# Output projection, norms and gate/up projection in one block, in token halves

## The reference

```python
hp = hp + rms_norm(mp, nw[1])
hs = hs + rms_norm(ms, nw[1])
hp = hp + rms_norm(swiglu(rms_norm(hp, nw[2]), ffn_w_gu[layer], ffn_w_down[layer]), nw[3])
hs = hs + rms_norm(swiglu(rms_norm(hs, nw[2]), ffn_w_gu[layer], ffn_w_down[layer]), nw[3])
```

## Time and profile before

| | us |
|---|---|
| median of 3 runs (1813.19 to 1816.3) | 1814.0 |
| the profiled execution | 1809.09 |
| its span, first to last instruction | 1807.4 |
| TensorE's matmuls busy in it | 1622.2 |

### The profile page before, as it was taken

One profiled execution on the slowest core, in us unless ns is written; L12 is line 12 of the kernel. 1 busy time (PEld: TensorE's weight loads), 2 busy tenths in 40 slices (PEclk: granted clock), 3 DMA queues, 4 the chain that ended last, 5 costly groups with the idle time before them and its releaser, 6 DMA issues. The chain is left out here.

```text
span 1807.4 us, 40950 instructions
## 1 busy us (share of the span) xinstructions
PE 1622.2 (90%) x16700; PEld 1511.5 (84%) x16700; DVE 811.6 (45%) x1344; ACT 498.0 (28%) x901; POOL 479.3 (27%) x406
## 2 busy tenths in 40 slices
PE   6998986999984999998997799999896999998994
PEld 5997974565584999998997799999695999998994
DVE  3332205565655444433233777675456344442334
ACT  3110004455532222221121433323233222221220
POOL 0001114576601344443000234342001444442001
PEclk9999798999996999998999899999798999999997
DMA  9655678687540222222221134343120222222211
GB/s 279 196 172 201 237 271 336 218 252 223 156 154 24 76 89 92 93 93 93 95 85 56 59 107 119 106 130 95 47 94 24 94 93 92 85 94 96 89 56 48
DMA packets 82982, 226.68 MB, mean 125 GB/s; under 512 B 17918, under 2 KB 18608, under 8 KB 81282
## 3 DMA queue, kind: packets, MB, share of 16 engines
q1 hardware_dynamic: 77522, 210.09, 35.4%
q0 software_dynamic: 3392, 11.02, 1.7%
q10 hardware_dynamic: 1936, 3.74, 0.6%
HBM read 206.28 MB, written 23.77 MB: 127 GB/s over the span
## 5 line engine op out<-in xcount | busy, mean ns | idle before, releaser
L370 PE MATMUL gu_ps<-gu_x_hi,gu_w_hi 128*128 128x260 f32 x1408 | 288.4, 286 | 38.3 <-DVE gu_x_lo L336 31.3
L370 PE MATMUL gu_ps<-gu_x_hi,gu_w_lo 128*128 128x260 f32 x1408 | 285.3, 284 | 0.0
L370 PE MATMUL gu_ps<-gu_x_lo,gu_w_hi 128*128 128x260 f32 x1408 | 284.8, 284 | 0.0
L370 PEld LDWEIGHTS gu_ps<-gu_x_hi,gu_w_hi 128*128 128x128 f32 x1408 | 219.7, 190 | 41.1 <-issue 40.0
L370 PEld LDWEIGHTS gu_ps<-gu_x_hi,gu_w_lo 128*128 128x128 f32 x1408 | 218.7, 190 | 0.0
L370 PEld LDWEIGHTS gu_ps<-gu_x_lo,gu_w_hi 128*128 128x128 f32 x1408 | 218.0, 189 | 0.0
L289 DVE TENSOR_TENSOR gu_w_lo<-ring,gu_w_hi 128x1024 fp32r<-128x1024 f32 x88 | 143.8, 1634 | 100.5 <-ACT gu_w_hi L262 100.5
L370 PE MATMUL down_ps<-ffn_h_hi,down_w_hi 128*128 128x260 f32 x704 | 143.7, 286 | 17.2 <-DVE down_w_lo L289 17.2
L1239 POOL TENSOR_SCALAR arena<-arena 128x128 f32<-128x128 f32 (+3 forms) x128 | 137.1, 1087 | 79.0 <-DVE arena L1370 78.9
L456 POOL TENSOR_TENSOR ffn_h_hi<-ffn_a,ffn_g 128x520 f32 (+1 forms) x44 | 59.4, 1349 | 319.7 <-DVE ffn_g L445 319.7
L370 PE MATMUL down_ps<-ffn_h_lo,down_w_hi 128*128 128x260 f32 x704 | 142.7, 284 | 0.0
(11 more groups left out here) (337 smaller groups left out, 2899.4 us busy)
## 6 DMA issues: line engine op xcount, KB each, us to landing
ring<-in_w_gu SPq DMA_DIRECT2D x88, 512.0 KB, 3.7
ring<-in_w_down SPq DMA_DIRECT2D x32, 704.0 KB, 4.0
arena<-in_cache_cmp SPq DMA_DIRECT2D x86, 256.0 KB, 5.0
ring<-in_hgrn_w_in SPq DMA_DIRECT2D x32, 512.0 KB, 3.9
X<-in_slc_kv SPq DMA_DIRECT2D x48, 256.0 KB, 3.4
ring<-in_nsa_w_in SPq DMA_DIRECT2D x21, 512.0 KB, 3.8
arena<-in_cache_cmp POOLq DMA_DIRECT2D x42, 256.0 KB, 5.6
ring<-in_slc_kv SPq DMA_DIRECT2D x40, 256.0 KB, 3.1
```

The source lines that it names most:

```text
L370: last = pe.matmul(ps[j][:, h, 0:TH], wt[:, s % 2, a], xt[:, x, h * TH:(h + 1) * TH], start=(sub == 0 and k == 0 and part == 0), stop=(sub ...
```

## The change

The output projection, the norm after the mixer, the norm before the feed-forward part and gate/up become one block per layer, `mix_ffn`. Output tiles 0 to 3 are computed as before. Tiles 4 to 7 are computed for the first 260 tokens, and then all four for the second 260, from four slots of split weights; two of these lie in memory of the hidden units that are written last. While TensorE is at the second halves, the first half of the tokens goes through the norm. Gate/up tiles 0 to 2 follow in the same way, first for half 0, then for half 1; tile 3 is the first for all tokens, and from tile 4 on the loop is as before. Every operation of both norms is on 260 columns, except the mean and root of the second norm. The squares of the output are made by ScalarE from PSUM and added by GpSimd, and GpSimd makes all additions to `X`. In layer 0 the queries lie in `XW`, and the attention's output is written over them; the input projection is written out without a loop for this. The clearing of semaphores after the mixer now comes ahead of the output projection.

```diff
+def repeat(eng, first, last, unrolled):
+
+    if unrolled:
+        yield from range(first, last)
+    else:
+        with eng.Fori(first, last) as i:
+            yield i
...
-                with eng.Fori(1, loops) as i:
+                for i in repeat(eng, 1, loops, unrolled):
...
+        eng.tensor_tensor(pairs((c.XW[:, n, :] if n < KC else HT[:, n - KC, :])), ps[j][:, :, 0:TH], pairs(c.rstd[:, :]),
+                          ALU.mult).then_inc(c.psum_free[j], 1)
...
+def mix_ffn(c, name, w_mix, w_gu, nxt, Y, post_w, scale, hidden, ffn, ssq, x_ready=None):
...
+    PRE, ROUNDS = 3, 2 * FF // RING
...
+        late = FF * T - 4 * KC * P
+        more_h, more_l = [carve(flat_h, late + x * 2 * KC * P, 2, KC * P) for x in range(2)]
+        sh, sl = [carve(flat_l, x * KC * T, KC, T) for x in range(2)]
...
+        mq = [c.ring[:, 2 * x:2 * x + 2, KC * P:KC * P + TH] for x in range(2)]
+        w_hi, w_lo = [[x[:, 0, :], x[:, 1, :], m[:, 0, :], m[:, 1, :]] for x, m in ((wh, more_h), (wl, more_l))]
...
+            for tile in range(8):
+                s = tile % RING
+                sp.wait_ge(c.lo_cut[s], done[s] + tile // RING + 1)
+                load_tile(sp, c, w_mix if tile < RING else w_gu, s, (tile + RING) % KC, KC)
...
+                    used(act, n)
+                    act.activation(mq[n % 2], ps[j][:, :, 0:TH], ACT.Square).then_inc(mixed_sq, 1)
+                    act.activation(pairs(Y[:, n, :]), ps[j][:, :, 0:TH], ACT.Copy).then_inc(c.psum_free[j], 1)
...
+            cut(-8, 0)
+            for k in range(KC):
+                act.activation(sh[:, k, :], Y[:, k, :], ACT.Copy).then_inc(s_hi, 1)
+            for n in range(1, RING):
+                cut(n - 8, n)
...
+            for n in range(RING):
+                if n == 0:
+                    act.wait_ge(s_lo, KC)
+                out(n)
+                cut(n - RING, n)
+            for n in range(RING, 8):
+                out(n, 0)
+            out(4, 1)
+            root(1, cols[0])
+            used(act, 4)
+            cut(0, 0)
+            for k in range(2):
+                x_cut(0, k)
+            out(5, 1)
+            used(act, 5)
+            cut(1, 1)
+            for k in range(2, 4):
+                x_cut(0, k)
+            out(6, 1)
+            used(act, 6)
+            cut(2, 2)
+            for k in range(4, 6):
+                x_cut(0, k)
+            out(7, 1)
+            used(act, 7)
+            cut(3, 3)
+            for k in range(6, KC):
+                x_cut(0, k)
+            for k in range(4):
+                square(0, k)
+            root(2, cols[1])
+            for k in range(4, KC):
+                square(0, k)
+            for k in range(KC):
+                x_cut(1, k)
+                square(1, k)
+            root(3, slice(0, T))
+            later(act, cut)
...
+            def mean(h):
+
+                dve.wait_ge(summed, h + 1)
+                own.link(dve.tensor_scalar(c.rstd[:, cols[h]], ps[3][:, h, 0:TH], 1.0 / D_MODEL, EPS, ALU.mult, ALU.add))
+                dve.reciprocal(c.rstd[:, cols[h]], c.rstd[:, cols[h]]).then_inc(inverse, 1)
...
+                t, n = cols[h], h * KC + k
+                if n >= 2:
+                    dve.wait_ge(x_new, n - 1)
+                dve.scalar_tensor_tensor(y[:, k % 2, t], Y[:, k, t], post_w[:, k:k + 1], c.rstd[:, t], ALU.mult, ALU.mult)\
+                   .then_inc(scaled, 1)
...
+                dve.wait_ge(x_hi, n + 1)
+                dve.scalar_tensor_tensor(xl[:, k, t], c.X[:, k, t], scale[:, k:k + 1], xh[:, k, t].bitcast(F32), ALU.mult,
+                                         ALU.subtract).then_inc(x_lo, 1)
...
+            cut(-8, 0)
+            for k in range(KC):
+                dve.wait_ge(s_hi, k + 1)
+                dve.tensor_tensor(sl[:, k, :], Y[:, k, :], sh[:, k, :].bitcast(F32), ALU.subtract).then_inc(s_lo, 1)
+            for n in range(1, RING):
+                cut(n - 8, n)
+            for n in range(RING):
+                used(dve, n)
+                cut(n - RING, n)
+            mean(0)
+            dve.wait_ge(rooted, 1)
+            dve.wait_ge(half_out, RING)
+            scaled_by(0, 0)
+            scaled_by(0, 1)
+            used(dve, 4)
+            cut(0, 0)
+            for k in range(KC):
+                rest_of(0, k)
+                if k + 2 < KC:
+                    scaled_by(0, k + 2)
+                if k in (1, 3, 5):
+                    n = k // 2 + 1
+                    used(dve, 4 + n)
+                    cut(n, n)
+            mean(1)
+            dve.wait_ge(rooted, 2)
+            for j in range(RING):
+                dve.wait_ge(c.psum_free[j], freed[j] + 2)
+            scaled_by(1, 0)
+            scaled_by(1, 1)
+            for k in range(KC):
+                rest_of(1, k)
+                if k + 2 < KC:
+                    scaled_by(1, k + 2)
+            dve.wait_ge(squares_added, 2 * KC)
+            own.link(dve.tensor_scalar(pairs(c.rstd[:, :]), ps[3][:, :, 0:TH], 1.0 / D_MODEL, EPS, ALU.mult, ALU.add))
+            dve.reciprocal(c.rstd[:, :], c.rstd[:, :]).then_inc(inverse, 1)
+            dve.wait_ge(rooted, 3)
+            later(dve, cut)
...
+            def update(h, k):
+
+                t, n = cols[h], h * KC + k
+                pool.wait_ge(scaled, n + 1)
+                pool.tensor_tensor(c.X[:, k, t], c.X[:, k, t], y[:, k % 2, t], ALU.add).then_inc(x_new, 1)
...
+            pool.memset(ssq[:, :], 0.0).then_inc(added, 1)
+            for n in range(RING):
+                add(n)
+            for n in range(RING, 8):
+                add(n, 0)
...
+            add(4, 1)
+            for k in range(2):
+                update(0, k)
+            add(5, 1)
+            for k in range(2, 4):
+                update(0, k)
+            add(6, 1)
+            for k in range(4, 6):
+                update(0, k)
+            add(7, 1)
+            for k in range(6, KC):
+                update(0, k)
+            for k in range(KC):
+                update(1, k)
...
+                for part, (wt, xt) in enumerate(((w_hi, hi), (w_hi, lo), (w_lo, hi))):
+                    for h in halves:
+                        mm = pe.matmul(bank[:, h, 0:TH], wt[slot][:, a], xt[:, k, cols[h]], start=(k == 0 and part == 0),
+                                       stop=(k == n - 1 and part == 2))
+                return mm
...
+                s = n % RING
+                for k in range(KC):
+                    if wait_source:
+                        pe.wait_ge(s_lo, k + 1)
+                    mm = products(ps[s], s, (sh, sl), k, halves)
+                    if n == RING and halves == (1,) and k == 3:
+                        pe.wait_ge(added, 9)
+                        pe.wait_ge(half_out, RING)
+                        token_sums(0, ssq[:, cols[0]], True, True).then_inc(summed, 1)
...
+            for n in range(RING):
+                pe.wait_ge(c.lo_cut[n], done[n] + 1)
+                pe.wait_ge(c.psum_free[n], freed[n])
+                mixer(n, wait_source=n == 0).then_inc(c.tile_done[n], 1)
...
+                pe.wait_ge(c.lo_cut[j], done[j] + 2)
+                pe.wait_ge(c.psum_free[j], freed[j] + 1)
+                mixer(n, (0,)).then_inc(half_done, 1)
+            for n in range(RING, 8):
+                mixer(n, (1,)).then_inc(c.tile_done[n % RING], 1)
+            for h in range(2):
+                for n in range(PRE):
+                    if h == 0:
+                        pe.wait_ge(c.lo_cut[n], done[n] + 3)
+                        if n == 0:
+                            pe.wait_ge(inverse, 1)
+                    else:
+                        pe.wait_ge(c.psum_free[n], freed[n] + 2)
+                        if n == 0:
+                            pe.wait_ge(inverse, 2)
+                    for k in range(KC):
+                        if n == 0:
+                            pe.wait_ge(x_lo, h * KC + k + 1)
+                            if h and k:
+                                add_squares(1, k - 1)
+                        mm = products(ps[n], n, (xh, xl), k, (h,))
+                        if h == 0 and n and k % 2:
+                            add_squares(0, (n - 1) * 4 + k // 2)
+                    if h:
+                        mm.then_inc(c.tile_done[n], 1)
+                        if n == 0:
+                            add_squares(1, KC - 1)
+                    if h == 0 and n == 0:
+                        pe.wait_ge(added, 13)
+                        pe.wait_ge(c.psum_free[3], freed[3] + 2)
+                        token_sums(1, ssq[:, cols[1]], True, True).then_inc(summed, 1)
+            pe.wait_ge(c.lo_cut[3], done[3] + 3)
+            pe.wait_ge(inverse, 3)
+            for k in range(KC):
+                mm = products(ps[3], 3, (xh, xl), k, (0, 1))
+            mm.then_inc(c.tile_done[3], 1)
...
-                    mm = pe.matmul(b[2][:, col:col + 16], HT[:, u, i * P:(i + 1) * P],
```

(18 more changed lines are left out.)

193 lines of the change are left out of this document (171 added, 22 removed).

## The result

| | us |
|---|---|
| kernel before, median of 4 runs (1813.2 to 1816.3) | 1815.1 |
| changed kernel, median of 4 runs (1784.1 to 1788.2) | 1784.84 |
| ratio, 95% interval | 0.9838 (0.9821 to 0.9855) |
| profiled executions, before and after | 1809.09, 1784.62 |
| their spans | 1807.4, 1783.0 |

A forecast was written before the change was run, and what follows sets the result against it. TensorE was taken as the bound, its stops around gate/up's first tiles as the target: (64.4 - 40.2) + (54.2 - 40.2) - 2.4 = 35.8 us saved, 1773.3 profiled or 1778 against the 1814.0 median; range 1765 to 1790.

The forecast's parts named there:

- Half 0: First 260 tokens through both norms: start -7.4 us from output projection's end, chunk pairs 4.35 (bounds 3.4, 4.8), end 10.0.
- Rival 1: Half operations of VectorE and GpSimd hinder each other little: 3.25 us a pair, 5.5 more saved per layer, 1767; chance 0.16.
- rival 2: GpSimd additions at their 0.87 us median, gaps losing the clock fully: about 5 us lost per layer, 1788; chance 0.15.
- Rival 3: Successive matmuls into one bank wait for each other: 672 matmuls cost 108 us, 1886; chance 0.03.
- Rival 4: An unpriced wait in the new order stops TensorE 10 us or more per layer: 1795 to no gain; chance 0.04.
- The second norm: Norm before gate/up: costs nothing, hidden under gate/up tiles 1 and 2; stops of 3.4 and 3.6 us ahead of tile 2 go.
- Entry: Start of the block after the attention, now behind a clearing of semaphores: costs 1.2 us per layer, 2.4 in all.
- Clock: Slow TensorE after the two new gaps in gate/up's first half tile: 0 to 2 us, taken as 1.2 per layer.
- Half 1: Second 260 tokens: sum at 10.8 us, first `x_lo` 3 after the root, last at 26.0; TensorE waits about 0.3.
- a sign of being wrong: Prediction would be wrong if, among other signs, half 1 ran behind TensorE by more than 1 us.
- All 44 tiles from tile 4 on are as before: Gate/up tiles from tile 4 on: unchanged by the edit, priced at nothing.
- the forecast's own: Range of whole-kernel time for the main forecast alone: 1772 to 1784 us, from pairs at 3.9 to 4.8; chance 0.62.

The follow-up runs named there:

- experiment 1: Changed kernel with VectorE's splits of gate/up tiles 2 and 3 moved out of half 0's chunks; 1783.2 us.
- experiment 3: Changed kernel with output tiles 4 to 7 not crossed: TensorE does both token halves of each tile in turn; 1794.9 us.
- experiment 7: Changed kernel with the splits of gate/up tiles 2 and 3 later and the additions to `X` on VectorE, not GpSimd; 1774.7 us.
- experiment 8: Changed kernel with 24 idle matmuls in each of TensorE's two gaps in gate/up's first half tile; 1787.0 us in one execution.
- experiment 12: Changed kernel with half 1's first high part ahead of the last of half 0's squares on ScalarE; 1784.3 us.
- experiment 6: Kernel before with only the attention's first input projection written straight instead of looped; 1821.2 us.
- experiment 9: Kernel before with 8 idle matmuls (16 TensorE instructions) ahead of gate/up of layer 0; 1818.6 us in one execution.
- experiment 10: Kernel before with 64 idle matmuls (128 TensorE instructions) ahead of gate/up of layer 0; 1832.0 us in one execution.
- experiment 4: Kernel before, unchanged, run again for a second profile; this execution took 1814.1 us.

## Why the prediction was right, and where it was off

**Right in its mechanism.** *Half 0* came as worked out: it started at -7.1 (forecast -7.4) and ended at 9.9 (10.0), with pairs of 4.25 (4.35). TensorE's matmuls stood still for 5.9 us in its first half tile in layer 0 and 5.4 in layer 1, the 11.3 of the table (7 forecast for each), in two stops of 2.4 to 2.8 us (3.2 forecast) and short ones. The reason holds too: experiments 1, 3 and 7 changed the two engines' work, and each pair followed the sum of it, less the small overlap. The 4.35 itself was a choice between 3.4 and 4.8, and that it met 4.25 is in part luck. Rival 1 (halves hinder little, 3.25 a pair) and rival 2 (over 10 us of waits in half 0) are out. *Rival 3* is out: 48 matmuls of a single half take 5.8 us, 0.12 apart. *Rival 4* is out: TensorE's table has no wait inside the output projection, and experiment 3 shows that the crossing hides 5.5 and 3.6 us. *The second norm* was hidden, the stop ahead of tile 2 gone. *Entry* (1.2 forecast): in layer 0 the first high part starts 501.10 - 499.46 = 1.64 us after the attention's last operation, where it was 0.51, so 1.1 more; in layer 1 the norm and the entry together took 1.3 more. *Clock*: 1.2 forecast, 1.3 and 1.7 by experiment 8.

**Off inside the block**, by 0.9 and 1.3 us: the step "Half 1". Its last rest came at 28.0 and not 26.0; the 1.2 allowed under *Clock* covers a part of this. Its sum came at 11.9 and not 10.8, since at half clock (0.50, windows above) the last two chunks and the sum take nearly twice as long; with the clock kept up (experiment 8) it came 0.7 earlier. Its first `x_lo` ended 3.8 after the root's end (14.6) and not 3, because ScalarE's four last squares of half 0 stood ahead of its high part and waited for TensorE's sums. I had counted the squares for TensorE only and not as work queued ahead of `x_hi` on ScalarE. TensorE's matmuls waited 1.0 us for the last chunks of half 1, not 0.3, which is just at the limit that the prediction had set as a sign of being wrong. Experiment 12 gives back 0.35 of it in layer 1.

**Off outside it**, by 9.2 us in the spans: the sentence "All 44 tiles from tile 4 on are as before" and the missing recurrence stage. That stage costs 4.9 more, and experiments 6, 9 and 10 produce the same without the new block. Of the remaining 4.3, 1.9 is clock: the output projection of layer 1 took 48.8 us at 0.95 for 47.7 at 0.97, the same work, and the last norm's sums 641 ns each for 382, its stretch 23.1 us for 22.2. The rest I haven't taken apart. What makes the recurrence stage longer stays open. Shown is that 16 instructions more on TensorE, in a stage far ahead of it, are enough.

**Luck in the number.** The time, 1784.8, is inside the stated range but 0.8 us outside the forecast's own, 1772 to 1784. The part of the range that it fell into was there for rival 2, which is out; what filled it were costs that no term of the sum had. And the miss is 11.4 us in the spans but only 5.5 in the medians. The first profile of the kernel before was 5 us short in the attention (experiment 4), and that of the changed kernel agreed with its median. So 5.9 of the 30.3 us saved are not in any stage of the table. They lie ahead of the first output matmul, whose start varied by 8 us among the profiles of the changed kernel and its variants. Whether the change shortens the attention at all was not shown.

## What to carry to other kernels

Where VectorE and GpSimd both work on the chain that TensorE waits for, add their times; then moving an operation to the engine on which it is shorter, or moving a weight split to where VectorE idles anyway, gains nearly what the sum says (4.1 and 4.5 us in two layers here), and rearranging the same work gained nothing in the one case tried. Of each engine's queue list what stands ahead of the next critical operation, squares for a sum included. Judge a small edit by marks inside its block: the time of the whole program moves by 5 us or more for reasons that have nothing to do with it, so where an edit stands upstream of a stage like this recurrence, with its many short matmuls, time it in two or three shifted versions.

## What the runs showed of the hardware

- With 16 more instructions on TensorE ahead of it, a stage that is itself unchanged took 288.8 us where it took 284.3 and 284.4, and with 128 more 291.1 (one profile each).
- Operations of VectorE and GpSimd on half the tokens lengthen each other as full ones do: VectorE's split is 1.22 us alone and 1.5 beside GpSimd, GpSimd's addition 0.74 alone and 1.3 beside the split, VectorE's scaling 0.48 and 0.97.
- With two stops of TensorE of 2.8 and 2.7 us in layer 0 the granted clock fell from 1.00 to 0.75 and then 0.50 in windows of four microseconds. In layer 1 it was 0.50 from 1350.7 to 1352.7, where the first stop, of 2.8 us, ends (1351.7) and the second has not begun. With 24 idle matmuls in each stop it stayed at 1.00.
